# A sparse-attention stage with scores three steps ahead, shorter probability buffers and re-ordered cell work

## The reference

```python
def block(args):                         # 128 queries at a time, 16 heads in 2 groups
    s = einsum(qi, ck) * scale + bias    # compressed keys: 63 of them
    p_c = softmax(where(valid_c, s, NEG_INF)) * any(valid_c)
    o_c = einsum(p_c, cv)
    imp = einsum(p_c, ov)                # importance of the 16 key blocks, summed over 8 heads
    _, idx = top_k(score(imp), 8)        # with forced blocks
    ...
    p_s = softmax(einsum(qi, k_sel) * scale + bias_sel)   # chosen blocks
    o_s = einsum(p_s, v_sel)
    ...
    p_w = softmax(einsum(qi, k_win) * scale + bias_win)   # last 512 keys
    o_w = einsum(p_w, v_win)
o = gate0 * o_c + gate1 * o_s + gate2 * o_w
```

## Time and profile before

| | |
|---|---|
| time, median of 3 runs | 2697.97 us (2696.21 to 2698.81) |
| the profiled execution | 2701.7 us, its span 2699.9 us |
| TensorE busy | 2539.3 us, 94% of the span |
| VectorE busy | 1778.3 us, 66% |
| GpSimd busy | 1196.2 us, 44% |
| ScalarE busy | 1117.3 us, 41% |

### The profile page before, as it was taken

How to read it: one execution, slowest core, us unless ns; L and a number is a source line. 1 busy time by engine, 2 the same in 40 slices (tenths; PEclk the granted TensorE clock), 3 DMA queues, 4 the chain that set the end, 5 groups by cost and what they waited for, 6 DMA issues and landing times. The chain is left out here.

```text
span 2699.9 us, 38376 instructions
## 1 busy us (share of the span) xinstructions
PE 2539.3 (94%) x14192; PEld 2032.9 (75%) x14192; DVE 1778.3 (66%) x2850; ACT 1117.3 (41%) x2156; POOL 1196.2 (44%) x920
## 2 busy tenths in 40 slices
PE   8999889999999999999978788989999999989999
PEld 5777667888887778778765565768778888877787
DVE  5544754577679999650255555656636777799993
ACT  4526543253334434231254444556523433434331
POOL 5452665245444444524044555534623444544441
PEclk8999999999999999999999898999999999999999
DMA  4010003224335443222411012343232333364431
GB/s 163 32 47 32 1 1 121 82 106 159 142 144 203 138 166 114 94 96 81 124 28 52 26 52 58 83 115 83 61 115 89 129 151 150 117 229 145 151 142 63
DMA packets 91199, 275.79 MB, mean 102 GB/s; under 512 B 9879, under 2 KB 39191, under 8 KB 76359
## 3 DMA queue, kind: packets, MB, share of 16 engines
q1 hardware_dynamic: 87464, 255.18, 27.5%
q10 hardware_dynamic: 3552, 18.18, 1.7%
HBM read 197.50 MB, written 73.86 MB: 101 GB/s over the span
## 5 line engine op out<-in xcount | busy, mean ns | idle before, releaser
L1651 PE MATMUL ps<-U_hi,RH 128*128 128x512 f32 x912 | 356.8, 391 | 13.3 <-DVE H L940 5.8
L1655 PE MATMUL ps<-U_lo,RH 128*128 128x512 f32 x912 | 355.6, 390 | 0.0
L1656 PE MATMUL ps<-U_hi,RL 128*128 128x512 f32 x912 | 355.5, 390 | 0.0
L1075 POOL TENSOR_TENSOR RL<-RAW,RH 128x512 fp32r<-128x512 f32 x112 | 154.8, 1382 | 399.4 <-ACT RH L779 399.4
L779 ACT ACTIVATE RH<-RAW 128x512 fp32r<-128x512 f32 x280 | 175.5, 628 | 295.0 <-PE ps L1656 287.9
L1532 POOL TENSOR_SCALAR PX<-PX,rinv,GATE 128x640 f32<-128x640 f32 (+7 forms) x256 | 197.5, 782 | 222.9 <-DVE rinv L3376 221.8
L1651 PE MATMUL ps<-U_hi,W_hi 128*128 128x512 f32 (+2 forms) x656 | 262.8, 401 | 14.5 <-DVE U_lo L2892 11.9
L1651 PE MATMUL ps<-SH,RH 128*128 128x512 f32 x656 | 256.8, 391 | 8.9 <-DVE H L938 4.0
L1656 PE MATMUL ps<-U_hi,W_lo 128*128 128x512 f32 (+2 forms) x656 | 258.9, 395 | 0.0
L1655 PE MATMUL ps<-U_lo,W_hi 128*128 128x512 f32 (+2 forms) x656 | 258.6, 394 | 0.0
L1656 PE MATMUL ps<-SH,RL 128*128 128x512 f32 x656 | 256.0, 390 | 0.0
(11 more groups left out here) (390 smaller groups left out, 5858.8 us busy)
## 6 DMA issues: line engine op xcount, KB each, us to landing
W_raw<-in_pieces SPq DMA_DIRECT2D x30, 1024.0 KB, 5.1
RAW<-in_pieces SPq DMA_DIRECT2D x28, 1024.0 KB, 4.9
RAW<-in_pieces SPq DMA_DIRECT2D x56, 512.0 KB, 7.8
hid_d<-HOA SPq DMA_DIRECT2D x24, 1024.0 KB, 3.9
hid_d<-HOB SPq DMA_DIRECT2D x24, 768.0 KB, 5.4
RHA<-hid_d SPq DMA_DIRECT2D x12, 1024.0 KB, 5.1
RHB<-hid_d SPq DMA_DIRECT2D x12, 768.0 KB, 6.6
U_rawh<-hid_d SPq DMA_DIRECT2D x12, 768.0 KB, 4.5
```

Of the source, the lines that this page charges most:

```text
L1075: G_.tensor_tensor(ring(RL[i], n), quarter(n, (B22, B11)[i - 5]), ring(RH[i], n).bitcast(F32), ALU.subtract).then_inc(u_lop.sem, 1)
L1651: m = mm(o, a_hi, b_hi, start=first, stop=False, skip_group_check=again)
L1655: mm(o, a_hi, b_lo, start=False, stop=False, skip_group_check=again)
L1656: return mm(o, a_lo, b_hi, start=False, stop=last, skip_group_check=again)
```

## The change

In the window branch `PX` is replaced by ten buffers `PW` of 640 columns, and everything up to `normalise` moves one step ahead: in step s TensorE computes the scores of step s+3 (of s+2 in the second branch; step 61 has none), `inverse` and `normalise` are those of steps s+2 and s+1. In the second branch these keep their distances.

The cell products stand behind the scores, ahead of the first `turn_p`, and `SEQ` follows. On VectorE `cmp_out`, `q_low` and `cmp_bias` stand between the two `bias` of a step. The cell work of GpSimd has lags 1, 4, 6 and 7 instead of 1, 4, 5 and 5, and the transposes and the product follow with lags 9, 10 and 11 instead of 6, 7 and 9; the importance and masks with lags 43 to 51 instead of 41 to 49. `stage_q` is cut in two halves and `turn_q` comes two steps earlier. The clearing of query rows is cut into four (steps 43, 51, 59, 67), and each `load_q` of the first four heads waits for its own. The splits of the two weight pieces move to steps 120 to 123.

```diff
         def query_of(s):
-            return [(p, h) for p in range(1, N_PAIR) for h in range(2) if s == 8 * p - 6 + h]
+            return [(p, h) for p in range(1, N_PAIR) for h in range(2) if s == 8 * p - 8 + h]
+        def scored_in(s):
+            return [t for t in ((s + 3,) if s + 3 < N_BR else (s + 2,)) if (t < N_BR) == (s + 3 < N_BR) and t < N_STEP]
+        def inverse_in(s):
+            return [s + 2] if s + 2 < N_BR else [s + 1] if N_BR <= s + 1 < N_STEP else []
+        def normalised_in(s):
+            return [s + 1] if s + 1 < N_BR else [s] if N_BR <= s < N_STEP else []
+        def prob(U):
+            if U < N_ALL // 2:
+                return PW[U % 10], U - 10
+            return PX[(U - N_ALL // 2) % 7], U - 7 if U - 7 >= N_ALL // 2 else min(N_ALL // 2 - 1, U - 5)
...
# SyncE
             save_mask(0)
-            sp.wait_ge(k_zero, 1)
             for k in range(2):
                 sp.wait_ge(t_sv[k], 128)
-            load_q(0)
-            load_q(1)
+                sp.wait_ge(q_zero, k + 1)
+                load_q(k)
...
-            sp.wait_ge(q_zero, 1)
             for k in range(2, 4):
                 sp.wait_ge(t_sv[k], 128)
-            load_q(2)
-            load_q(3)
+                sp.wait_ge(q_zero, k + 1)
+                load_q(k)
...
# GpSimd
+            normalise(0)
+            normalise(1)
             for s in range(N_STEP):
-                normalise(2 * s)
-                normalise(2 * s + 1)
+                for t in normalised_in(s):
+                    normalise(2 * t)
+                    normalise(2 * t + 1)
                 if cell(s, 1) is not None:
                     below_max(cell(s, 1))
                 if cell(s, 4) is not None:
                     share(cell(s, 4))
-                if cell(s, 5) is not None:
-                    add_up(cell(s, 5))
-                    gate_p(cell(s, 5))
+                if cell(s, 6) is not None:
+                    add_up(cell(s, 6))
+                if cell(s, 7) is not None:
+                    gate_p(cell(s, 7))
...
# TensorE
+            scores(2)
             for s in range(N_STEP + 1):
-                if s + 2 < N_STEP:
-                    scores(s + 2)
+                for t in scored_in(s):
+                    scores(t)
+                if cell(s, 11) is not None:
+                    cmp_weigh(cell(s, 11))
...
+                for h in range(2):
+                    for g in imp_of(s, 50 + h):
+                        imp_mask(g, h)
+                for e in range(2):
+                    if cell(s, 9 + e) is not None:
+                        cmp_turn(cell(s, 9 + e), e)
+                for p, h in query_of(s):
+                    turn_q(p, h)
...
+                if cell(s, 0) is not None:
+                    cmp_scores(cell(s, 0))
                 if s < N_STEP:
                     turn_p(2 * s)
...
                 if s:
                     weigh_p(s - 1)
                 if s < N_STEP:
                     turn_p(2 * s + 1)
-                if cell(s, 9) is not None:
-                    cmp_weigh(cell(s, 9))
...
# VectorE
             for s in range(N_STEP + 1):
-                if 2 * s + 4 < N_ALL:
-                    bias(2 * s + 4)
-                if s + 1 < N_STEP:
-                    inverse(s + 1)
-                if 2 * s + 5 < N_ALL:
-                    bias(2 * s + 5)
+                if s + 2 < N_BR:
+                    inverse(s + 2)
+                for t in scored_in(s):
+                    bias(2 * t)
+                if s + 2 >= N_BR:
+                    for t in inverse_in(s):
+                        inverse(t)
+                if cell(s, 11) is not None:
+                    cmp_out(cell(s, 11))
...
                 for p, h in query_of(s):
                     q_low(p, h)
...
+                if cell(s, 0) is not None:
+                    cmp_bias(cell(s, 0))
+                for t in scored_in(s):
+                    bias(2 * t + 1)
...
```

More of the change, by code:

```diff
@@ L252, in build_program @@
         PX = [at("PX%d" % k, o, [P, S]) for k, o in enumerate([W0 + 1024 * k for k in range(4)] + [G0 + 1024 * k for k in range(3)])]
+        PW = [at("PW%d" % k, o, [P, RW]) for k, o in enumerate([W0 + RW * k for k in range(6)] + [G0 + RW * k for k in range(4)])]
         KVD = at("KVD", A0 + 8192, [P, NT, 4, P])
@@ L347, in build_program @@
         gd_in = sem("gains_in")
-        k_sc, k_tr, k_hi, k_lo, k_cp, k_zero = (sem("nsa_k_" + x) for x in "scaled tr hi lo copied zero".split())
+        k_sc, k_tr, k_hi, k_lo, k_cp = (sem("nsa_k_" + x) for x in "scaled tr hi lo copied".split())
         q_zero = sem("q_rows_zero")
@@ L606, in rot, with last_in @@
         def rot(*x):
-            return 4 + NO[x] % 2
+            return ROT[NO[x]]
+        def last_in(b, n):
+            return max((m for m in range(n) if ROT[m] == b), default=-1)
         def emptied(n):
@@ L1513, in _ @@
             pool.wait_ge(h_rs, 2 + 3)
-            stage_q(0)
-            stage_q(1)
+            stage_q(0, 0)
+            stage_q(0, 1)
+            stage_q(1, 0)
+            stage_q(1, 1)
             pool.wait_ge(c_mm, 1)
@@ L2244, in _ @@
                     turn_p(2 * s + 1)
-                if cell(s, 9) is not None:
-                    cmp_weigh(cell(s, 9))
-                for g in imp_of(s, 41):
-                    imp_turn(g, 0)
-                    imp_turn(g, 1)
-                for e in range(2):
-                    if cell(s, 6 + e) is not None:
-                        cmp_turn(cell(s, 6 + e), e)
-                for h in range(2):
-                    for g in imp_of(s, 48 + h):
-                        imp_mask(g, h)
-                if cell(s, 0) is not None:
-                    cmp_scores(cell(s, 0))
             out_proj(P_OUT1, 1, XL0)
@@ L2706, in _ @@
             key_high(7)
+            expo(4)
+            expo(5)
             for s in range(N_STEP + 1):
+                for g in imp_of(s, 43):
+                    imp_turned(g, 0)
+                    imp_turned(g, 1)
+                for h in range(2):
+                    for g in imp_of(s, 50 + h):
+                        mask_turned(g, h)
+                for e in range(2):
+                    if cell(s, 9 + e) is not None:
+                        cmp_turned(cell(s, 9 + e), e)
+                for p, h in query_of(s):
+                    q_high(p, h)
+                if s == 2:
+                    ck_high()
                 if s < N_STEP:
                     copy_p(2 * s)
-                for p, h in query_of(s):
-                    q_high(p, h)
-                if s == 1:
-                    ck_high()
-                for U in (2 * s + 4, 2 * s + 5):
-                    if U < N_ALL:
-                        expo(U)
+                for t in scored_in(s):
+                    expo(2 * t)
+                if s % 4 == 0 and 0 < s <= N_BR:
+                    window_out(s // 4 - 1)
+                for t in scored_in(s):
+                    expo(2 * t + 1)
                 if cell(s, 2) is not None:
                     cmp_exp(cell(s, 2))
-                for g in imp_of(s, 41):
-                    imp_turned(g, 0)
-                    imp_turned(g, 1)
-                for e in range(2):
-                    if cell(s, 6 + e) is not None:
-                        cmp_turned(cell(s, 6 + e), e)
-                for h in range(2):
-                    for g in imp_of(s, 48 + h):
-                        mask_turned(g, h)
-                if s % 4 == 0 and 0 < s <= N_BR:
-                    window_out(s // 4 - 1)
             act.wait_ge(x_qk, N_ALL)
@@ L3256, in key_low @@
                 j, g, half = n // 4, n // 2 % 2, n % 2
-                cols, b = slice(half * HALF, (half + 1) * HALF), 6 + m if m < 2 else rot("k", m)
+                cols, b = slice(half * HALF, (half + 1) * HALF), rot("k", m) if m else 7
                 hi, lo, rows = ((KS2, KSS, slice(DK, P)), (KW2, KWS, slice(0, P)))[j]
@@ L3444, in _ @@
                     cmp_clamp(cell(s, 5))
-                for part in range(6):
-                    for g in imp_of(s, 42 + part):
+                for part in range(1, 6):
+                    for g in imp_of(s, 44 + part):
                         choose(g, part)
@@ L3449, in _ @@
                     copy_p(2 * s + 1)
-                if cell(s, 9) is not None:
-                    cmp_out(cell(s, 9))
-                if cell(s, 0) is not None:
-                    cmp_bias(cell(s, 0))
                 if s % 4 == 0 and s > N_BR:
```

132 lines of the change are left out of this document (71 added, 61 removed).

## The result

The changed kernel takes 2648.99 us (median of 4 runs, 2644.14 to 2653.65) where the kernel before took 2698.01 in the same session: ratio 0.9819, 95% interval 0.9801 to 0.9837. That is 49.0 us less; 42 were forecast. The profiled execution took 2644.14 us.

What follows compares the result with a forecast made beforehand. TensorE, busy 94% of the span, was taken as the bound, losing time to window-branch waits and slow clock. Terms -50 + 1 + 2 + 5 + 0 = -42 us on 2701.7 gave 2659.7, adjusted to the median: 2656 us; range 2630 to 2688.

Steps and rivals of the forecast that it cites:

- The window branch: Window branch of the attention loop: GpSimd waits, bank waits and slow clock go, short bank waits come; gains 50 us.
- the pair: One pair of heads in the window branch: 36.5 us instead of 44.3, including 4.5 us of new waits.
- One step of lead covers it: Window branch: normalise issued a step before turn_p hides GpSimd's delay; all 22.8 us of waits go.
- with the long waits the slow stretches: Window branch: stretches at the lower clock vanish once TensorE's long waits go; 24 us gained.
- The start: Start of the attention loop: two more bias ahead of the first inverse cost +1 us, between 0 and 2.
- The clearing of query rows: Last clearing, moved to step 67, delays head 3's loads for scores(72): +2 us, between 0 and 6.
- The second mask: Mask transpose 5.4 us later makes scores(88) wait 5 us longer, 11.5 in all; bounds 3 and 7.
- The splits: Weight splits near the end: two waits of some 2.4 us replace 3.72 and a short one; 0, -4 to +3.
- The clock keeps falling: Rival: waits go but nine short ones a pair keep bringing the lower clock; 2680 us, chance 0.15.
- `q_low` holds up VectorE: Rival: q_low between the two bias waits for q_high, delaying the scores; slower, 2716 us, chance 0.09.
- It doesn't do what it says: Rival: normalise stays late behind below_max and bank waits are exchanged one for one; near 2706 us, chance 0.05.
- nearly all waits vanish: Rival: as if only 1 us of waits stayed per pair of heads; 2630 us, chance 0.06.

Runs made afterwards that it cites:

- the spread: GpSimd's add_up and gate_p at lags 6 and 7 instead of one block with below_max; undone in the changed kernel: 2650.6 us, ratio 0.9823.
- run with the products ahead: Changed kernel with cell products ahead of their step's scores on TensorE and, on VectorE, the pieces reading them ahead of both bias: 2673.2 us, ratio 0.9891.
- the place: Cell products behind the scores, with VectorE's readers between both bias; kept in the changed kernel with three-step lead and GpSimd's cell-work spreading undone: 2704.0 us, ratio 1.0022.
- the last version: Changed kernel with scores two steps ahead, queries of heads 6 and 7 loaded before saving the second mask, second key transpose in bank 6: 2629.0 us, ratio 0.9736.
- run with two steps of lead: Changed kernel with window-branch scores, inverse and normalise back at their old distances (scores two steps ahead, normalise in its own step): 2642.3 us, ratio 0.9798.
- the early loads: Changed kernel with SyncE issuing queries and bias rows of heads 6 and 7 ahead of saving the second mask: 2632.9 us, ratio 0.9755.
- a late `q_low`: Changed kernel with ScalarE doing each q_high of pairs 1 to 7 four times, ahead of q_low, in 14 places: 2701.1 us, ratio 0.9997.
- the single wait of 2.82 us: Seen in the changed kernel with three-step lead and spreading of GpSimd's cell work undone, cell products still behind the scores: 2704.0 us, ratio 1.0022.
- only the rest of the change was left: Changed kernel with three-step lead, spreading of GpSimd's cell work and new position of the cell products all undone: 2741.9 us, ratio 1.0145.
- VectorE's readers first: Changed kernel with cmp_out, q_low and cmp_bias ahead of both bias on VectorE, TensorE's order kept: 2660.3 us, ratio 0.9836.

## Why the prediction was right, and where it was not

**The window branch** (-50, measured -59). The steps were: GpSimd's waits go (22.8, now 0.3), the bank waits go and short ones come, the slow clock goes (24 estimated; busy time fell by 20.4). The direction and the places were right, `turn_p` behind `q_low` among them. What was mis-sized is the pair: 36.5 us forecast, 35.39 measured. I had worked out 3.4 us of waits and taken 4.5; they are 2.61. The first and last steps gave some 5 us instead of 3 (59.0 less 6.07 pairs of 8.92).

**Its reasons were half wrong.** "One step of lead covers it" is true, but the spread covers it as well, and either would have done. And "with the long waits the slow stretches" was read as GpSimd's waits alone, because the pair shown had one of 1.67 us in front of its slow stretch; the bank wait of 0.98 us ahead of it and the wait of 1.89 us that left the clock alone were passed over. The run with the products ahead has no wait for GpSimd and 18.7 us more of busy time than the changed kernel. So the clock's 20 us were a gain of the place together with the lead or the spread, and of VectorE's new order, which I had counted only as a risk. That the sum came out near is in part luck: with all edits made at once, it did not have to know which of them removes which wait.

**The start** (+1 within 0 to 2, measured +4.8) is the term that failed outright. Two `bias` were counted, but not the wait of the second `turn_k` for a bank that `q_low` empties (2.5 us, of which 1.6 reach the end, as the last version shows), nor that the fourth scores, which now stand ahead of the first `turn_p`, wait 2.28 us for a `bias`. The run with two steps of lead gives back 3.2 us of the 4.8. The lower clock of the last pair of `turn_k` (3.59 us) explains none of this difference: with two steps of lead they take 3.63 us.

**The clearing of query rows** (+2, measured no wait at the scores of step 72; the stretch up to them became 3.0 us shorter). I had let the old and the new bank waits of these steps cancel; the old ones were larger (2.9 us against 1.4), and 1.4 us of waits for `normalise` went that I had not counted in this branch.

**The second mask** (+5, wait 11.5). The wait is 11.38, and the stretch 6.5 us longer, half of it busy time (3.3 us), since the clock of the stretch is 0.92 instead of 0.98. The number was right, and so was the chain from the transpose to the scores as it ran. But I took it as given: one link, that these queries follow the second mask, is only SyncE's order, as the early loads showed, and 13.5 us could be had there.

**The splits**: 0 forecast and measured, two waits of 2.28 and 1.38 us for one of 3.72 and a short one.

**The rivals.** *The clock keeps falling* did not come true: 0.99. *`q_low` holds up VectorE* did not come true either: VectorE waits 4.4 us at `q_low` instead of 30.7, with `turn_q` earlier and `q_high` ahead of `copy_p` on ScalarE. Its price is real, by another path: with 37.5 us of waits for the bank that `q_low` empties the kernel is as slow as the kernel before. *It doesn't do what it says* and *nearly all waits vanish* are out: 23.6 us of idle time stay.

The Trainium skill's section on cycling through PSUM banks ("TensorE: Matmul & The Clock Gate", A second HAM failure mode: psum-queue depth-cycling) tells of a kernel in which short idling between groups, with the banks cycled in each iteration, made the clock swing. In the changed kernel it doesn't: the banks turn in every step, with 23.6 us of idle time in waits of at most 1.1 us behind the first steps, and the clock is 0.99. With the products ahead it does: the clock is 0.92, with bank waits and hardly any others. So what the Trainium skill tells there is seen in the one arrangement and not in the other.

## What to carry to other kernels

Two cures for one wait don't add up: before crediting a gain to one of them, undo each alone, since here a lead that took ten new buffers was worth nothing beside two pieces of cell work put into later steps. Where TensorE's clock is in play, read busy time and idle time of the same work apart: the 30 us of waits that a late `q_low` added made the window part 57 us longer, and behind the single wait of 2.82 us nearly 20 us of work went at half the clock. And where a load is late, ask first what stands ahead of it in its queue, not what it seems to wait for.

## What was not expected of the hardware

The same idle time can go with very different clocks: 62.1 us of idle in the window part with 268.4 us busy in the kernel before, 64.2 us with 298.6 us busy where only the rest of the change was left.

No single length of a wait tells whether the clock falls. In the kernel before 1.89 us left it alone where 1.67 us, with a bank wait just ahead, did not. Busy time by stretch in the changed kernel, around a wait of 1.13 us behind `q_low`:

```profile
1402.00:1405.00 3.00, 1.87 (x15) 1.23 (x15) 2.46 (x7) 2.48 (x6) 0.00 (x0) 1.00 0.00 0
1405.00:1408.00 3.00, 2.96 (x32) 2.17 (x32) 2.46 (x6) 1.69 (x5) 1.81 (x2) 1.00 0.91 249
```

And with VectorE's readers first, around a wait of 1.10 us for `bias`:

```profile
1511.00:1514.00 3.00, 1.87 (x16) 0.80 (x13) 2.34 (x6) 1.33 (x5) 3.00 (x5) 1.00 0.01 3
1514.00:1517.00 3.00, 3.00 (x21) 2.67 (x21) 1.10 (x5) 1.39 (x4) 3.00 (x4) 0.58 0.00 0
```

TensorE is busy 1.87 of 3 us in both, and the clock is 1.00 behind the one and 0.58 behind the other.

And in the changed kernel the one fall that is left in the window part behind its first steps follows no wait longer than 0.26 us, but the importance sum, 16 products of 16 columns, and twelve of `cmp_scores`. TensorE's timeline, and the busy time by stretch:

```profile
1557.84 1.96 PE L2161 MATMUL ps<-cs,KVD 63*128 63x16 f32 x16 [0.26 <-DVE PT L3419]
...
1561.82 2.40 PE L2237 MATMUL ps<-PT,KV 128*64 128x128 f32 x20
```

```profile
1559.00:1562.00 3.00, 3.00 (x26) 2.65 (x27) 1.27 (x5) 0.01 (x1) 0.24 (x1) 0.91 0.03 5
1562.00:1565.00 3.00, 3.00 (x24) 2.54 (x23) 0.27 (x3) 1.69 (x5) 0.00 (x0) 0.52 0.45 119
```

That these products bring the fall is not shown. With two steps of lead the same products run in the same order behind a wait of 0.20 us, and the clock stays at 1.00; the same `weigh_p` there:

```profile
1561.98 1.31 PE L2235 MATMUL ps<-PT,KV 128*64 128x128 f32 x20
```

What a wait, or a row of small products, must be like for the clock to fall stays open here.
